# Two inner norms applied behind the products, in a transformer step on one core

## Chip, core and metric

The kernel runs on one core of a Trainium2 chip. TensorE multiplies into PSUM, VectorE (DVE) and ScalarE (ACT) do the elementwise work, GpSimd (POOL) a few selects, and SyncE (SP) issues nearly all loads. Each engine works through its own queue of instructions in order; they meet through semaphores. The metric is the device time of one execution in microseconds.

## What is computed

One inference step of a two-layer decoder on 288 tokens (256 of a prompt, 8 x 4 of running sequences), width 1024, fp32. Layer 0 is sparse attention and a dense SwiGLU, layer 1 a gated gMLP and a top-2-of-8 expert SwiGLU. Cut to what matters here:

```python
def rms_norm(x, g):
    y = xf * lax.rsqrt(jnp.mean(xf * xf, axis=-1, keepdims=True) + EPS)
    return (y * g.astype(jnp.float32)).astype(x.dtype)
def swiglu(h, w_gate, w_up, w_down):
    return (jax.nn.silu(h @ w_gate) * (h @ w_up)) @ w_down
def gmlp_mixer(h, w_in, ln_g, ln_b, w_s, b_s, w_out):
    u, v = jnp.split(jax.nn.gelu(h @ w_in, approximate=False), 2, axis=-1)
    v = layer_norm(v, ln_g, ln_b)
    ...
    return (u * mixed.reshape(B, T, GM_WIDTH)) @ w_out, v
xp = xp + op.reshape(B, S, -1) @ attn_w_out[j]
xp = xp + swiglu(rms_norm(xp, norm_ffn[i]), ffn_w_gate[j], ffn_w_up[j], ffn_w_down[j])
op, _ = gmlp_mixer(rms_norm(xp, norm_mix[i]), ...)
```

The two inner norms are the one ahead of the dense SwiGLU (n = 1) and the one ahead of the gMLP (n = 2).

## The kernel before

The residual stream `xT` lies transposed, 8 chunks of 128 features by 288 tokens. A dense product is made in three: each operand is split into a high part (rounded to `fp32r`) and a low part (the rest), and `three()` (L1660) adds high x high, high x low and low x high. `project_split` makes a block of 128 output columns from 8 chunks, 24 products. `project_tokens_split` has the tokens as the stationary side, and works through a quarter of the weights (2 chunks) at a time for three tiles of tokens, 18 products.

Weights come in tiles of 2 MB through a ring of 7 slots. A tile has four quarters. ScalarE copies the head of a quarter into one of `WD` = 3 buffers `wd` (`heads_before`, L754), as soon as TensorE has read the quarter three before it (`d_used`); VectorE subtracts it in place to get the tail (`tails_before`, L1150). Where the calls `heads_before(n)` and `tails_before(n)` stand in each engine's program sets the order of this work against the rest. `F0`, `FD0`, `GV0`, `GU0`, `GO0` number the first quarters of gate and up, down, the gMLP's v and u halves and its output.

Results land in six PSUM banks in turn (`A`), named ("wo", m) for the attention output, ("fg", f) and ("fu", f) for gate and up, ("fd", m) for down, ("gv", m, half), ("gu", c), ("mix", g); `room` makes TensorE wait until the bank six names earlier is freed. The sums of squares use two more banks (`B`).

An inner norm, before: VectorE adds each block to `xT` (`residual`, L1390). After the last, ScalarE and VectorE square half of the stream each (L791, L1164), `ssq` (L1643) sums over features with eight fp32 products with `ones`, ScalarE takes the root into `rt` (L793), VectorE the reciprocal (L1166) and then, chunk by chunk, weight times norm (L1168, into `hL`), ScalarE the high part `hT_r` (`h_heads`), VectorE the low part `hL_r` (`h_tail_of`, L1158). Only then has TensorE its operand. In the FFN loop ScalarE makes Silu of the gate block from PSUM (L969) and VectorE the product with the up block (L1407), whose high and low parts are `hh` and `hhl_r` (L1400). Ahead of the second norm ScalarE issues five loads of parameters (L979 to L983). In the gMLP the v half goes through Gelu (L992), statistics (L1429), roots (L1003) and a layer norm on VectorE (L1448 to L1451) while TensorE makes the u half, whose Gelu is at L1000. The mix adds its bias at L1458.

## Time and profile before

| | us |
|---|---|
| median of 3 runs (lowest, highest) | 1683.6 (1681.77, 1691.64) |
| the profiled execution | 1692.52 |
| its span, first to last instruction | 1690.8 |
| busy: TensorE, its weight loads | 1618.4 (96%), 1377.8 (81%) |
| busy: VectorE, ScalarE, GpSimd | 1237.8 (73%), 986.6 (58%), 54.5 (3%) |
| mean granted TensorE clock | 0.971 |

The attention stages fill the first 303 us, the FFN runs to 530, the gMLP to 646, and the eight experts take the rest. A timeline row is start, length, engine, line, operation, output and inputs; the bracket at its end says how long the engine had idled before it, and what released it. L1660 is the line of all split products, L754 of all copies on ScalarE, whose output tells them apart.

### The profile page before, as it was taken

The page shows a single profiled execution, that of the slowest core. Times are in us where ns is not written, and L with a number is a line of the kernel's source. Part 1 is how long each engine was busy: PE and PEld are TensorE (multiplying, and loading weights), DVE is VectorE, ACT ScalarE, POOL GpSimd, SP SyncE. Part 2 cuts the span into 40 slices and gives each one's busy share as a digit, 9 for nine tenths or more (in the row PEclk, how much of TensorE's full clock was granted, in tenths as well). Part 3 has the DMA queues.
Part 4 walks back from the last instruction along what each step waited for, and adds up shares of the span by engine and source line. Part 5 has one row for each costly group of instructions (what it writes and reads, how often), then busy time and mean ns, then how long its engine had stood idle before and what let it go on. Part 6 is the DMA issues. An engine that isn't in the chain of part 4 may idle for free.

```text
span 1690.8 us, 22113 instructions
## 1 busy us (share of the span) xinstructions
PE 1618.4 (96%) x8441; PEld 1377.8 (81%) x8441; DVE 1237.8 (73%) x1168; ACT 986.6 (58%) x933; POOL 54.5 (3%) x62
## 2 busy tenths in 40 slices
PE   7998989899996998899999999999999999999998
PEld 6886978799996787788888888888888888888886
DVE  4586353455533484888998988998998988988986
ACT  2443342344432445677777767767767777777774
POOL 3520000000000000000000000000000000000000
PEclk9999689999998999999999999999999999999999
DMA  7194236153645232699999999999999999999980
GB/s 235 69 349 157 100 123 227 50 175 126 223 150 200 84 119 100 250 350 346 361 356 345 373 349 345 371 346 343 380 344 343 367 356 342 362 356 350 365 292 29
DMA packets 194264, 444.17 MB, mean 263 GB/s; under 512 B 10841, under 2 KB 13947, under 8 KB 194203
## 3 DMA queue, kind: packets, MB, share of 16 engines
q1 hardware_dynamic: 190082, 436.91, 71.5%
q10 hardware_dynamic: 4120, 6.42, 1.1%
q8 instruction: 41, 0.67, 0.2%
q14 instruction: 21, 0.16, 0.0%
HBM read 439.57 MB, written 3.74 MB: 262 GB/s over the span
## 4 chain that ended last, share of the span: by engine, by line
PE 90%; DVE 6%; ACT 1%; issue 1%; ACTq 1%; DMA 0%; DVEq 0%
PE bank L1660 20%; PE bank L2065 12%; PE bank L2067 12%; PE bank L2066 12%; PE bank L2075 6%; PE bank L2077 6%; PE bank L2076 6%; PE bank L1652 3%; PE bank L1831 2%; PE bank L2083 1%; PE bank L2038 1%; DVE rt L1292 1%; PE bank L1821 1%; PE bank L2053 1%; PE bank L2054 1%
## 5 line engine op out<-in xcount | busy, mean ns | idle before, releaser
L1499 DVE TENSOR_TENSOR wql<-ring,wqh 128x2048 fp32r<-128x2048 f32 x336 | 767.6, 2288 | 112.4 <-ACT wqh L754 109.3
L754 ACT ACTIVATE wqh<-ring 128x2048 fp32r<-128x2048 f32 x336 | 646.2, 1924 | 261.0 <-PE bank L2067 172.2
L2065 PE MATMUL bank<-wqh,xgh 128*128 128x512 f32 x896 | 357.5, 399 | 4.2 <-DVE wql L1499 2.5
L2067 PE MATMUL bank<-wqh,xgl 128*128 128x512 f32 x896 | 350.8, 392 | 0.0
L2066 PE MATMUL bank<-wql,xgh 128*128 128x512 f32 x896 | 350.2, 391 | 0.0
L1150 DVE TENSOR_TENSOR ring_r<-ring,wd 128x1024 fp32r<-128x1024 f32 x90 | 109.9, 1224 | 140.5 <-ACT wd L754 140.5
L2065 PEld LDWEIGHTS bank<-wqh,xgh 128*128 128x128 f32 x896 | 169.1, 189 | 38.6 <-DVE wql L1499 3.4
L2067 PEld LDWEIGHTS bank<-wqh,xgl 128*128 128x128 f32 x896 | 169.0, 189 | 36.5
L2066 PEld LDWEIGHTS bank<-wql,xgh 128*128 128x128 f32 x896 | 169.3, 189 | 33.1
L1660 PE MATMUL bank<-hT_r,ring_r 128*128 128x288 f32 x608 | 180.8, 297 | 0.0
L2075 PE MATMUL bank<-wqh,heTh 128*128 128x512 f32 x448 | 175.1, 391 | 1.9 <-DVE heTl L1499 1.9
L2077 PE MATMUL bank<-wqh,heTl 128*128 128x512 f32 x448 | 175.0, 391 | 0.0
L2076 PE MATMUL bank<-wql,heTh 128*128 128x512 f32 x448 | 174.8, 390 | 0.0
L754 ACT ACTIVATE wd<-ring 128x1024 fp32r<-128x1024 f32 x90 | 94.9, 1057 | 117.2 <-PE bank L1660 117.1
L1660 PE MATMUL bank<-hT_r,wd 128*128 128x288 f32 x480 | 143.9, 300 | 8.5 <-DVE hL_r L1158 5.8
L1660 PE MATMUL bank<-hL_r,wd 128*128 128x288 f32 x480 | 143.4, 299 | 0.0
L1660 PEld LDWEIGHTS bank<-hT_r,ring_r 128*128 128x128 f32 x608 | 116.0, 191 | 0.0
L1660 PEld LDWEIGHTS bank<-hT_r,wd 128*128 128x128 f32 x480 | 92.5, 193 | 11.9 <-issue 6.4
L2075 PEld LDWEIGHTS bank<-wqh,heTh 128*128 128x128 f32 x448 | 84.5, 189 | 19.7 <-DVE wql L1499 2.2
L2076 PEld LDWEIGHTS bank<-wql,heTh 128*128 128x128 f32 x448 | 84.5, 189 | 17.6
L2077 PEld LDWEIGHTS bank<-wqh,heTl 128*128 128x128 f32 x448 | 84.4, 188 | 17.6
L1660 PEld LDWEIGHTS bank<-hL_r,wd 128*128 128x128 f32 x480 | 92.0, 192 | 0.0
(331 smaller groups left out, 1906.2 us busy)
## 6 DMA issues: line engine op xcount, KB each, us to landing
ring<-in_moe_w_gate SPq DMA_DIRECT2D x56, 2048.0 KB, 8.2
ring<-in_moe_w_up SPq DMA_DIRECT2D x56, 2048.0 KB, 8.1
ring<-in_moe_w_down SPq DMA_DIRECT2D x56, 2048.0 KB, 8.3
ring<-in_attn_w_in SPq DMA_DIRECT2D x7, 2048.0 KB, 10.2
ring<-in_ffn_w_gate SPq DMA_DIRECT2D x5, 2048.0 KB, 8.6
ring<-in_ffn_w_up SPq DMA_DIRECT2D x5, 2048.0 KB, 7.8
ring<-in_cache_k SPq DMA_DIRECT2D x16, 512.0 KB, 13.0
ring<-in_cache_v SPq DMA_DIRECT2D x16, 512.0 KB, 5.6
```

Of the source, the lines that this page charges most:

```text
L754: return nc.scalar.activation(dst, src, ACT.Copy)
L1150: v.tensor_tensor(in_tile(n, ring_r), in_tile(n), its_heads(n).bitcast(F32), ALU.subtract)\
L1499: return v.tensor_tensor(dst, src, head.bitcast(F32), ALU.subtract)
L1652: last = mm(A.ap(group)[0:width, 0:ncols], tile[:, c, col:col + width], rhs[:, c, 0:ncols], start=(c == 0), stop=(c == k - 1))
L1660: return mm(out, w, x, **flags) if weights_stay else mm(out, x, w, **flags)
L1831: last = mm(B.ap("st")[:, c0:c0 + TS], KT[:, n % 2, h, :], qT[:, h, NP + TS * b:NP + TS * b + TS], start=True, stop=True)
L2065: mm(bank, xgh[:, k, :], w_h[:, part], start=(k == 0), stop=False)
L2066: mm(bank, xgh[:, k, :], w_l[:, part], start=False, stop=False)
L2067: last = mm(bank, xgl[:, k, :], w_h[:, part], start=False, stop=(k == KD - 1))
L2075: mm(bank, heTh[:, left], w_h[:, part], start=first, stop=False)
L2076: mm(bank, heTh[:, left], w_l[:, part], start=False, stop=False)
L2077: last = mm(bank, heTl[:, left], w_h[:, part], start=False, stop=final)
```

## The change

A row's norm is a factor per token, and a product is linear in it. So the change feeds the products with the stream times weight only, not divided, and multiplies the results. For the SwiGLU both results are multiplied by `rt` on VectorE, the gate ahead of Silu. For the v half the factor lies along partitions, so it is the `scale` of the Gelu on ScalarE (`rk`); for the u half VectorE multiplies by `rt` ahead of Gelu. High and low parts of the weighted stream are made behind each residual add: the high part on ScalarE straight from `xT`, the low part on VectorE in one instruction. ScalarE squares each chunk, VectorE keeps a running sum in `rt`, and TensorE sums over features with one product with `ones`, put after the first block of the stage (for n = 2 with three small ones that give the factor per token row). Line numbers below are not those of before.

```diff
-        def squares_and_root(n, xt_ready):
...
+        def raw_heads(n, name, chunks, dst):
+            for m in chunks:
+                act.wait_ge(*A.freed((name, m)))
+                nc.scalar.activation(dst[:, m, :], xT[:, m, :], ACT.Copy, scale=gT[:, 8 * n + m:8 * n + m + 1])\
+                  .then_inc(h_head, 1)
+                k = KD * (n - 1) + m
+                if k >= 2:
+                    act.wait_ge(usum_ok, k - 1)
+                nc.scalar.activation(usq[:, m % 2, :], xT[:, m, :], ACT.Square).then_inc(usq_ok, 1)
...
-        squares_and_root(1, A.freed(("wo", KD - 1)))
-        h_heads(h_ready, KD)
+        raw_heads(1, "wo", range(KD), hU)
+        nc.scalar.activation(rk[0:1, 3:4], epst[0:1, 0:1], ACT.Sqrt)
         for f in range(NFB):
...
             heads_before(F0 + 2 * f + 1 + WD)
+            if f == 0:
+                act.wait_ge(*B.full(("ssq", 1)))
+                nc.scalar.activation(rt[:], B.ap(("ssq", 1))[:, 0:T], ACT.Sqrt, bias=epst[:, 0:1], scale=1.0 / D)\
+                  .then_inc(b_act, 1)
+            act.wait_ge(*A.freed(("fg", f)))
+            nc.scalar.activation(sg[:, f % 2, :], sg[:, f % 2, :], ACT.Silu).then_inc(silu_ok, 1)
...
         hidden_head(NFB - 1)
+        heads_before(first_of["fd", 1, 0] + WD - 1)
+        raw_heads(2, "fd", range(4), hT_r)
+        heads_before(GV0 + WD - 1)
+        raw_heads(2, "fd", range(4, KD), hT_r)
         heads_before(GV0 + WD)
+        nc.scalar.activation(rk[0:1, 3:4], epst[0:1, 0:1], ACT.Sqrt)
...
-        squares_and_root(2, A.freed(("fd", KD - 1)))
-        h_heads(h_ready, 2 * KD)
+        heads_before(GV0 + QU + WD - 1)
+        act.wait_ge(*B.full(("ssq", 2)))
...
+        act.wait_ge(ln_ok, 1)
+        nc.scalar.activation(mv[:, 0:2, 2:3], mv[:, 0:2, 1:2], ACT.Sqrt, bias=epst[:, 0:1])
...
         for c in range(KD):
             heads_before(GU0 + c + 1 + WD)
-            act.wait_ge(*A.full(("gu", c)))
...
+            act.wait_ge(*A.freed(("gu", c)))
+            nc.scalar.activation(gu[:, c, :], gu[:, c, :], ACT.Gelu).then_inc(gelu_ok, 1)
...
+        def raw_tail(n, m, heads):
+            turned[0] += 1
+            dve.wait_ge(h_head, turned[0])
+            v.scalar_tensor_tensor(out=hL_r[:, m, :], in0=xT[:, m, :], scalar=gT[:, 8 * n + m:8 * n + m + 1],
+                                   in1=heads[:, m, :].bitcast(F32), op0=ALU.mult, op1=ALU.subtract).then_inc(h_tail, 1)
...
+                v.tensor_tensor(rt[:], rt[:], usq[:, m % 2, :], ALU.add).then_inc(usum_ok, 1)
...
         for f in range(NFB):
+            dve.wait_ge(*A.full(("fg", f)))
...
+            v.tensor_tensor(sg[:, f % 2, :], A.ap(("fg", f))[:, 0:T], rt[:], ALU.mult).then_inc(a_dve, 1)
             tails_before(F0 + 2 * f + 1 + WD)
-            dve.wait_ge(*A.full(("fu", f)))
-            dve.wait_ge(*A.freed(("fg", f)))
-            v.tensor_tensor(hhl[:, f, :], sg[:, f % 2, :], A.ap(("fu", f))[:, 0:T], ALU.mult).then_inc(a_dve, 1)
             if f >= 1:
                 hidden_tail(f - 1)
+            dve.wait_ge(*A.full(("fu", f)))
+            v.tensor_tensor(hhl[:, f, :], A.ap(("fu", f))[:, 0:T], rt[:], ALU.mult).then_inc(a_dve, 1)
+            dve.wait_ge(*A.freed(("fu", f)))
+            dve.wait_ge(silu_ok, f + 1)
+            v.tensor_tensor(hhl[:, f, :], hhl[:, f, :], sg[:, f % 2, :], ALU.mult).then_inc(prod_ok, 1)
             tails_before(F0 + 2 * f + 2 + WD)
         hidden_tail(NFB - 1)
-        tails_before(first_of["fd", 1, 0] + WD)
...
+        tails_before(first_of["fd", 1, 0] + WD - 1)
+        for half in range(2):
+            for m in range(4 * half, 4 * half + 4):
+                residual("fd", m)
+                if m > 4 * half:
+                    raw_tail(2, m - 1, hT_r)
+            raw_tail(2, 4 * half + 3, hT_r)
+            if half == 0:
+                tails_before(GV0 + WD - 1)
...
-        def ssq(n):
+        def sum_of_squares(n):
+            bank = B.ap(("ssq", n))
             B.room(pe, ("ssq", n))
...
+            pe.wait_ge(usum_ok, KD * n)
+            last = mm(bank[:, 0:T], ones[:], rt[:], start=True, stop=True)
...
-            for m in range(4):
-                A.room(pe, ("fd", 4 * half + m))
...
                         for m in range(4):
+                            if f == 0:
+                                A.room(pe, ("fd", 4 * half + m))
```

Where the instructions stand, at three places. First VectorE from the end of the attention output on, before (L1390 residual, L1164 squares, L1168 and L1158 the normed chunk and its low part):

```order
L1150 TENSOR_TENSOR ring_r<-ring,wd 128x8x128 x3
L1390 TENSOR_TENSOR xT<-xT,bank 128x288 x8
L1164 TENSOR_TENSOR hT<-xT 128x1152
L1166 RECIPROCAL rt<-rt 128x288
L1168 SCALAR_TENSOR_TENSOR hL<-xT,gT,rt 128x288 x2
L1158 TENSOR_TENSOR hL_r<-hL,hT_r 128x288
```

and now, from the last residual add (L1410) to the second pair of the FFN loop (L1186 low part, L1194 running sum, L1172 tail of a quarter, L1433 gate times norm, L1438 up times norm, L1441 product with Silu):

```order
L1410 TENSOR_TENSOR xT<-xT,bank 128x288
L1186 SCALAR_TENSOR_TENSOR hL_r<-xT,gT,hU 128x288
L1194 TENSOR_TENSOR rt<-rt,sg 128x288
L1186 SCALAR_TENSOR_TENSOR hL_r<-xT,gT,hU 128x288
L1194 TENSOR_TENSOR rt<-rt,sg 128x288
L1172 TENSOR_TENSOR ring_r<-ring,wd 128x8x128
L1421 RECIPROCAL rt<-rt 128x288
L1433 TENSOR_TENSOR sg<-bank,rt 128x288
L1438 TENSOR_TENSOR hhl<-bank,rt 128x288
L1441 TENSOR_TENSOR hhl<-hhl,sg 128x288
L1172 TENSOR_TENSOR ring_r<-ring,wd 128x8x128
```

The low part of chunk 6 stands behind the last residual add, and the reciprocal behind one more tail.

Second, ScalarE from the end of the down projection on, before:

```order
L754 ACTIVATE wd<-ring 128x1024 x22
L979 DMA wr<-in_moe_w_router 128x8x8
L980 DMA wsr<-in_gm_w_s 128x8x128
L981 DMA lng<-in_gm_ln_g 128x1024
L982 DMA lnb<-in_gm_ln_b 128x1024
L983 DMA bsb<-in_gm_b_s 128x1024
L791 ACTIVATE hT<-xT 128x1152
L793 ACT_TABLE_LOAD
L793 ACTIVATE rt<-bank,epst 128x288
L754 ACTIVATE hT_r<-hL 128x288 x8
L754 ACTIVATE wd<-ring 128x1024 x4
L992 ACT_TABLE_LOAD
```

and now, from the last weighted copy (L798) and square (L803):

```order
L798 ACTIVATE hT_r<-xT,gT 128x288
L803 ACTIVATE sg<-xT 128x288
L760 ACTIVATE wd<-ring 128x1024
L992 ACT_TABLE_LOAD
L992 ACTIVATE rk<-epst 1x1
L996 DMA wr<-in_moe_w_router 128x8x8
L997 DMA wsr<-in_gm_w_s 128x8x128
L998 DMA lng<-in_gm_ln_g 128x1024
L999 DMA lnb<-in_gm_ln_b 128x1024
L1000 DMA bsb<-in_gm_b_s 128x1024
L760 ACTIVATE wd<-ring 128x1024 x3
L1005 ACTIVATE rk<-bank,epst 128x2
```

The five DMAs stand behind the weighted copies, between the head of quarter 2 of the v half and those of quarters 3, 4 and 5.

Third, VectorE in the gMLP after the statistics, now (L1492 u block times norm, L1481, L1484, L1486 the layer norm's three steps; before, the nine of them and three tails came in a row, with no L1492):

```order
L1492 TENSOR_TENSOR gu<-bank,rt 128x288
L1172 TENSOR_TENSOR ring_r<-ring,wd 128x8x128
L1484 TENSOR_TENSOR gv<-gv,lng 128x1024
L1486 TENSOR_TENSOR gv<-gv,lnb 128x1024
L1492 TENSOR_TENSOR gu<-bank,rt 128x288
L1172 TENSOR_TENSOR ring_r<-ring,wd 128x8x128
L1481 TENSOR_SCALAR gv<-gv,mv 128x1024
L1484 TENSOR_TENSOR gv<-gv,lng 128x1024
```

Each tail now stands behind two steps of the norm at most, and the roots on ScalarE stand ahead of its first head of this stage.

## Rows read from the trace of the kernel before

**Rows 1.** The page's second part, granted clock in 40 slices
```profile
PEclk9999689999998999999999999999999999999999
```
**Rows 2.** The timeline around the first inner norm
```profile
303.36 0.45 DVE L1390 TENSOR_TENSOR xT<-xT,bank 128x288 f32<-128x288 f32 x1 [3.43 <-PE bank L1652]
...
305.35 5.81 PE L1643 MATMUL bank<-hT,ones 128*128 128x288 f32 x16 [2.03 <-DVE hT L1164]
...
311.73 1.95 DVE L1166 RECIPROCAL rt<-rt 128x288 f32<-128x288 f32 x1 [6.53 <-ACT rt L793]
...
315.12 0.51 DVE L1168 SCALAR_TENSOR_TENSOR hL<-xT,gT,rt 128x288 f32<-128x288 f32 x1
...
315.35 0.38 PE L1660 MATMUL bank<-hT_r,wd 128*128 128x288 f32 x1 [4.19 <-DVE hL_r L1158]
...
324.42 1.06 ACT L754 ACTIVATE wd<-ring 128x1024 fp32r<-128x1024 f32 x1 [1.65 <-PE bank L1660]
...
324.49 0.45 DVE L1407 TENSOR_TENSOR hhl<-sg,bank 128x288 f32<-128x288 f32 x1 [0.46 <-PE bank L1660]
```
**Rows 3.** The chain of waits in order of time: start, length, what, instructions
```profile
37.35 3.47 PE bank L1732 x32
...
270.35 32.98 PE bank L1652 x128
...
320.05 171.43 PE bank L1660 x1301
...
586.47 0.87 PE bank L1975 x8
```
**Rows 4.** The timeline between the halves of the down projection
```profile
491.56 1.06 ACT L754 ACTIVATE wd<-ring 128x1024 fp32r<-128x1024 f32 x1 [2.12 <-PE bank L1660]
...
494.86 0.37 PE L1660 MATMUL bank<-hh,wd 128*128 128x288 f32 x1 [3.26 <-DVE xT L1390]
```
**Rows 5.** The timeline around the second inner norm
```profile
534.91 2.80 ACTq L981 DMA_DIRECT2D lng<-in_gm_ln_g  x1
...
538.73 1.16 ACT L791 ACTIVATE hT<-xT 128x1152 f32<-128x1152 f32 x1 [7.63 <-issue]
...
539.99 6.36 PE L1643 MATMUL bank<-hT,ones 128*128 128x288 f32 x16 [9.91 <-ACT hT L791]
...
551.33 0.76 PE L1660 MATMUL bank<-wd,hT_r 128*128 128x512 f32 x1 [4.99 <-DVE hL_r L1158]
...
557.17 1.06 ACT L754 ACTIVATE wd<-ring 128x1024 fp32r<-128x1024 f32 x1 [1.89 <-PE bank L1660]
...
561.33 1.06 ACT L754 ACTIVATE wd<-ring 128x1024 fp32r<-128x1024 f32 x1 [3.11 <-PE bank L1660]
```
**Rows 6.** The timeline of the gMLP's u half
```profile
588.57 1.28 DVE L1429 BATCH_NORM_STATS2 bn<-gv 128x6 f32<-128x512 f32 x2
...
600.73 0.81 DVE L1448 TENSOR_SCALAR gv<-gv,mv 128x1024 f32<-128x1024 f32 x1
...
601.38 1.28 ACT L1000 ACT_TABLE_LOAD   x1
...
601.57 1.23 DVE L1450 TENSOR_TENSOR gv<-gv,lng 128x1024 f32<-128x1024 f32 x1
...
602.67 0.41 ACT L1000 ACTIVATE gu<-bank 128x288 f32<-128x288 f32 x1
...
605.34 0.37 PE L1660 MATMUL bank<-hT_r,wd 128*128 128x288 f32 x1 [1.86 <-DVE ring_r L1150]
...
619.65 0.41 DVE L1458 TENSOR_TENSOR hL<-bank,bsb 128x256 f32<-128x256 f32 x1
```
**Rows 7.** Busy time by stretch: length, PE, PEld, DVE, ACT, POOL, clock, DMA share
```profile
606.00:609.50 3.50, 3.50 (x17) 3.50 (x16) 3.47 (x4) 0.00 (x0) 0.00 (x0) 0.52 0.41 150
690.00:1000.00 310.00, 310.00 (x1407) 255.84 (x1405) 274.72 (x173) 224.40 (x154) 0.00 (x0) 1.00 0.98 355
```
**Rows 8.** The timeline, a later weighted copy of one chunk
```profile
634.11 0.54 ACT L1025 ACTIVATE uT<-xT,gT 128x288 f32<-128x288 f32 x1 [1.66 <-DVE xT L1390]
```

More of the change, by code:

```diff
@@ L1395, in _ @@
             residual("wo", m)
-        norm(1, A.freed(("wo", KD - 1)), hL)
+            if m:
+                raw_tail(1, m - 1, hU)
+        raw_tail(1, KD - 1, hU)
+        tails_before(F0 + 1 + WD)
+        dve.wait_ge(*B.freed(("ssq", 1)))
+        v.reciprocal(rt[:], rt[:]).then_inc(r_ok, 1)
+        dve.wait_ge(r_ok, 1)
         def hidden_tail(f):
@@ L1455, in _ @@
+        for _ in norming:
+            pass
         for g in range(8):
```

147 lines of the change are left out of this document (76 added, 71 removed).

## Prediction

> **What bounds the kernel now.** I read the page first. The line of the granted clock is near full speed but for the fifth and sixth slice, ahead of the change [rows 1], so the body runs on a busy TensorE and only stretches where it stops can be won. Next the chain of waits in order of time: between 270 and 645 us it is nearly all TensorE. The stretches of it give prices per product: 64 fp32 products (two instructions each) of the attention output take 32.98 us, 0.52 each; 1301 split products take 171.43 us, 0.132 each, so a block of 24 is 3.16 us; 16 fp32 products of 8 columns take 3.47 us, 0.22 each [rows 3]. Then the timeline for the places where TensorE idles. There are five in reach of the change.
>
> A: the first inner norm. The last residual add starts at 303.36, TensorE does eight fp32 products with `ones` for 5.81 us, ScalarE takes the root, VectorE a reciprocal of 1.95 us, and TensorE stands still for 4.19 us ahead of its first split product. The first product of gate and up comes on VectorE at 324.49 [rows 2]. So 21.1 us pass from the end of the attention output (303.33) to the end of the second FFN block (324.42), which itself holds two blocks, 6.3 us.
>
> B: between the halves of the down projection, 3.26 us idle. The fifth block of 128 columns waits until VectorE has made one more low part and then all four residual adds [rows 4].
>
> C: the second inner norm. TensorE stops at 530.08 (539.99 less 9.91), because ScalarE issues five DMAs (one of them for 2.80 us) before it squares, at 538.73. Then come 6.36 us of sums and 4.99 us idle until 551.33 [rows 5]. The next stage, eight quarters of 18 products, ends at 586.47 [rows 3]; undisturbed a quarter takes 4.17 us, as the head copies of 557.17 and 561.33 stand apart [rows 5].
>
> D: the u half of the gMLP, where VectorE normalises v between its low parts: 1.86 us idle at 605.34, then the clock at 0.52 for 3.5 us [rows 6, 7].
>
> After that comes the expert stage, with TensorE busy 310 of 310 us at full clock while the DMA engines are busy 98% [rows 7]. Each transfer there waits for a ring slot that the products free, so the stage should shift as a whole.
>
> **The change, part by part.** Times below count from the end of the TensorE work ahead of a place. A semaphore takes about 0.05 us (324.42 to 324.49 has one). A VectorE row that waits for nothing starts some 0.08 us before its predecessor ends. The weighted copy on ScalarE is 0.54 us [rows 8]. The square of a chunk I take as 0.44 us, as a copy less its scale operand; the bounds are 0.41 and 0.54. A product and subtraction in one VectorE instruction is 0.51, an add 0.45, the residual's [rows 2].
>
> *A.* Per chunk VectorE has residual add, low part and running sum, 0.45 + 0.51 + 0.45 = 1.4 us; ScalarE has 0.54 + 0.44. An attention output block takes 8 x 0.52 = 4.1 us, so chunks 0 to 6 hide, except that the tail of chunk 6 stands behind residual 7 in VectorE's queue (order rows above). That tail ends at 0.9, chunk 7's at 1.8. TensorE asks for chunk 6 at 18 x 0.132 = 2.4 and for chunk 7 at 2.8: no wait. Block 1 ends at 3.16, one fp32 product with `ones` replaces eight, 0.52, the second block ends at 6.84. Behind it: head of quarter 3 3.15 to 4.2, root to 4.7, tail to 5.45, reciprocal to 7.4, three products with the norm and the gate until 8.9, head and tail of quarter 4 until 10.7, wanted at 13.2. So A goes from 21.1 to 6.8: **14.3 us**.
>
> *FFN loop.* Two more VectorE products per block pair, 22 x 2 x 0.45 = 20 us of work, are costed at nothing: they lie beside 6.32 us of TensorE per pair, in which VectorE then has two low parts of 1.23 and four products and differences of 0.45, 4.3 us. The latest item is the tail of the quarter behind the Silu product. After the up block is full (3.16): scaled up 3.65, product with Silu 4.1, and the tail (its head done at 4.2) 5.4, wanted at 6.32: slack 0.9 us. Silu itself is done at 1.5 and not waited for. Without this cover each us of lateness would cost 22 us.
>
> *B.* The tail that stood ahead of the adds is now behind them, and the room is asked for by block. Residuals 0 and 1 end at 0.5 and 0.9; TensorE comes to blocks 6 and 7 at 0.8 and 1.2. Late next is the low part of the third quarter: ScalarE's four weighted copies and squares follow VectorE's 1.3 us per chunk and end at 4.55, head to 5.6, tail to 6.85; wanted at 6.32. So 3.26 becomes 0.55: **2.7 us**.
>
> *C.* The bank of the third token tile waits for residual 4: start at 0.5. Quarters 0 and 1 need chunks 0 to 3, made at B; chunks 4 to 7 are done at 5.2, wanted from 8.9. ScalarE then has the head of quarter 2 (to 5.6), the table and the dummy root (to 7.1), the DMAs (4.9, to 12.0) and only then the head of quarter 3, 13.05, tail 14.3. TensorE wants it at 0.5 + 3 x 4.17 = 13.0: a new wait of 1.3. Sums: 0.52 + 3 x 0.22 = 1.2. Root, reciprocals (1.95 + 0.3) and `rk` are ready for Gelu by 23 and hidden by the second half; the first bank that Gelu frees is wanted at 36. So C takes 0.5 + 33.4 + 1.3 + 1.2 = 36.4 instead of 586.47 - 530.08 = 56.4: **20.0 us**.
>
> The DMA issue is the term with far bounds. It is at least 2.5 us (2.80 less any waiting, the four short ones stay) and at most 4.9 plus the 8 us that the ring tile issued at the same moment could hold the queue; I take 4.9 as measured, with the same traffic around it. The low bound removes the wait (gain 1.3 more), the high one makes it some 8.
>
> *Table load.* The dummy root costs 1.28 + 0.2 us here. In the rows the table load of 1.28 us at 601.38 was followed by its activation at 602.67 at once [rows 6]. The Trainium skill, "ScalarE: Activation LUTs", section "What ACT_TABLE_LOAD costs", adds a drain of about 1.38 us to every switch; by that rule the head of quarter 3 would be 1.4 us later still and C 18.6. This case's trace doesn't show the drain, so the sum goes by the trace.
>
> *D.* VectorE is the bound between the end of the v stage (0) and the first mix add: 33.2 us in before (619.65 - 586.47). Now: statistics from 2.1 to 6.4 (1.28 a pair, plus 0.16 as I take it for each aggregate), one product, then a wait for the two roots and the next head (8.1), tail and reciprocals to 9.65, and nine norm rows (0.81 and twice 1.23 three times over, 9.8) [rows 6], seven products (2.7), seven tails (8.1) and the sample weights (nine tiny instructions, 1.0 as I take it): 31.1, overlaps of 0.08 taken off. All eight products of TensorE find their low part ready; it waits at the mix instead. Gain **2.0 us**, bounds 0 and 3.5 (1.86 and the slow clock).
>
> Sum 14.3 + 2.7 + 20.0 + 2.0 = 39.0 us. The profiled execution took 1692.5 us (span 1690.8), so 1653.5; it is 8.9 above the median of the runs, which gives 1683.6 - 39.0 = **1644.6 us**.
>
> **The rivals.**
> 1. *A wait takes the place of the sums (gain 27 to 35 us, about 1653).* Place: quarter 3 of C, behind ScalarE's DMAs, and the clock behind each short stop. For it: a stop of 1.86 us was followed by 3.5 us at 0.52, which cost 1.7 us [rows 6, 7]; three new short stops (B, C, mix) at that price cost 5, and a queue held 3 us longer costs 3. Against it: the stop of 3.26 us at B has no slow rows behind it. By the Trainium skill, "TensorE: Matmul & The Clock Gate", section "A second HAM failure mode: psum-queue depth-cycling", frequent micro-idling makes the clock swing between its levels; the wait rows here bear that out once in two.
> 2. *The expert stage gives it back (within 1%).* For it: DMA at 98% from 690 to 1000 us. If the weights were the bound, the earlier start would win nothing beyond the tiles already in the ring. Against it: TensorE idles 0 us there; transfers are paced by slots it frees. Time then between 1668 and 1683.
> 3. *Slower: the FFN's VectorE queue.* The tail stands behind a wait for ScalarE's Silu. If round trip and queue end more than 0.9 us later than worked out, each pair loses the rest; at 0.9 + 39.0 / 22 = 2.7 us late the gain is gone, at 3.7 the time is 1683.6 + 22 = 1706. For it: VectorE's share rises from half of the stage to two thirds. Against it: its rows are 0.45 us and Silu is done 2 us before.
>
> **How the numbers follow.** Forecast (gain 35 to 42) 0.72, rival 1 0.20, rival 2 0.05, rival 3 beyond no gain 0.02, a smaller loss there 0.01. The range reaches from the low bound of the DMAs and of D (-1.3, -1.5, and 4 for the state of the chip, since three runs lie 10 us apart) to rival 1: 1637 to 1657. About 1% is what a measurement of this kernel can tell from no change: faster 0.93 (gain above 17), same 0.05, slower 0.02.
>
> **What would show it.** TensorE should pass from the attention output to the FFN without a stop, with one `ones` product between its first two blocks; the gMLP's v stage should start within 1 us of the down projection and pause once, before its fourth quarter, ahead of which ScalarE's queue shows the DMAs; the FFN loop should keep 0.132 us a product (if not: rival 3); the expert stage should keep TensorE busy throughout (if not: rival 2). The prediction is wrong if the low clock follows the new stops for more than 3.5 us each.

## The result, and the profile after

| | before | after |
|---|---|---|
| median us (runs) | 1687.62 (1681.77, 1683.6, 1691.64, 1692.54) | 1642.54 (1641.32, 1642.12, 1642.96, 1643.46) |
| ratio | | 0.9734, 95% interval 0.9708 to 0.976 |
| profiled execution, its span | 1692.52, 1690.8 | 1642.12, 1640.4 |
| mean granted clock | 0.971 | 0.984 |

The kernel is faster; the forecast was 1644.6 us, with a range of 1637 to 1657. The kernel before was run 25 more times beside the experiments (medians 1683.47, 1684.47 and 1684.84), so its median in the table is some 4 us high; against 1684 the change is worth 42 us, a ratio of 0.975. One thing has to be taken out of the difference of the two spans, 50.4 us, before it is read. The attention output starts at 260.50 us in the profile of after and at 270.35 in that of before, in code that the change does not touch (`rk` moves its tiles by 32 bytes, too). That is 9.85 us, and the clock accounts for it: the fifth and sixth slice of the page (169 to 254 us in before, 164 to 246 in after) stand at 6 and 8 in before [rows 1] and at 9 and 8 in after. Up to that start the mean granted clock is 0.91 in before and 0.95 in after, and 270.35 x 0.91 and 260.50 x 0.95 are 246 and 247 us of full clock. The other 40.5 us lie behind that point, where the change is. From here on, "behind attention" is the span less the start of the attention output: 1420.45 us in before, 1379.9 in after.

The page of after, its busy times and its granted clock:

```profile
PE 1594.5 (97%) x8419; PEld 1359.7 (83%) x8419; DVE 1257.1 (77%) x1220; ACT 993.0 (61%) x951; POOL 54.6 (3%) x62
...
PEclk9999989999999998999999999999999999999999
```

The chain of waits of after in order of time (start, length, what, instructions), around the first inner norm and then around the second:

```profile
294.09 3.18 PE bank L1718 x24
297.27 0.49 PE bank L1696 x2
297.76 14.25 PE bank L1718 x107
```

```profile
500.00 21.95 PE bank L1718 x112
521.95 0.48 PE bank L1696 x2
522.44 0.50 PE bank L1700 x6
522.94 16.57 PE bank L1718 x71
```

Where [rows 2] has eight products with `ones`, a stop of 4.19 us and the first split product at 315.35, there is now one product (two instructions, L1696) between the first two blocks, and no stop. Where [rows 5] has stops of 9.91 and 4.99 us around 6.36 us of sums, the second chain runs through: one product of 288 columns and three of 8 (L1700). From 294 to 566.57 us TensorE never stands still for more than 0.04 us, and its granted clock is 1.00; in before it is 0.96 from 303.3 to 586.3 us and 0.88 in C alone, so a part of the gains at A and C is clock that the stops no longer cost. The one new stop is at the mix, where the forecast had it. In the timeline of after:

```profile
567.48 0.38 PE L2050 MATMUL bank<-wsT,gv 128*128 128x128 f32 x1 [0.90 <-DVE gv L1486]
```

The clock stays at 1.00 behind it, up to 600 us.

Stage by stage, from the timelines of both (us):

| stretch | before | after | gain | forecast |
|---|---|---|---|---|
| A: end of the attention output to end of the second FFN block | 21.1 | 6.8 | 14.3 | 14.3 |
| rest of the FFN loop, and down | | | 1.3 | 2.7 (B), loop 0 |
| of it B, the stop between the halves | 3.26 | 0 | 3.3 | 2.7 |
| C: end of down to the transposes | 56.2 | 34.3 | 22.0 | 20.0 |
| D: transposes to the first mix addition | 33.3 | 30.8 | 2.5 | 2.0 |

C and D are taken here from the first transpose of the timeline, 586.30 in before and 539.57 in after, 0.17 us ahead of where the chain [rows 3] has it. The table leaves one loss: B alone gave 3.3, the whole stretch 1.3, so the loop took 2 us more. It shows in VectorE's scaling of each gate block, here two pairs in a row of after's timeline:

```profile
348.98 0.46 DVE L1433 TENSOR_TENSOR sg<-bank,rt 128x288 f32<-128x288 f32 x1 [0.95 <-PE bank L1718]
...
355.38 0.46 DVE L1433 TENSOR_TENSOR sg<-bank,rt 128x288 f32<-128x288 f32 x1 [0.95 <-PE bank L1718]
```

A pair takes 6.40 us; in before, 6.29 on average over 17 pairs. TensorE stops in neither, so each product has become slower, 0.1333 us instead of 0.1311.

The timeline of after around the second norm, ScalarE and the DMA issues (ACTq and SPq are the queues of ScalarE and SP that issue them):

```profile
505.33 0.37 SPq L641 DMA_DIRECT2D ring<-in_moe_w_gate  x1
...
507.83 0.54 ACT L798 ACTIVATE hT_r<-xT,gT 128x288 fp32r<-128x288 f32 x1 [0.29 <-DVE xT L1410]
507.98 0.41 ACTq L996 DMA_DIRECT2D wr<-in_moe_w_router  x1
508.27 0.43 ACT L803 ACTIVATE sg<-xT 128x288 f32<-128x288 f32 x1
508.42 0.60 ACTq L997 DMA_DIRECT2D wsr<-in_gm_w_s  x1
508.61 1.05 ACT L760 ACTIVATE wd<-ring 128x1024 fp32r<-128x1024 f32 x1
509.05 3.93 ACTq L998 DMA_DIRECT2D lng<-in_gm_ln_g  x1
509.67 1.28 ACT L992 ACT_TABLE_LOAD   x1
510.96 0.20 ACT L992 ACTIVATE rk<-epst 1x1 f32<-1x1 f32 x1
513.00 0.46 ACTq L999 DMA_DIRECT2D lnb<-in_gm_ln_b  x1
513.49 0.45 ACTq L1000 DMA_DIRECT2D bsb<-in_gm_b_s  x1
514.04 2.01 ACT L760 ACTIVATE wd<-ring 128x1024 fp32r<-128x1024 f32 x2 [2.88 <-PE bank L1718]
```

Down ended at 505.30. The forecast had these in a row: square, head, table and dummy root until 7.1 us behind that, then 4.9 us of issues, then the head of quarter 3 at 12.0. The rows show the issues beside the engine's work, and that head at 8.74.

### The profile page after: what moved, and what is told of

Read it like the earlier page. It is cut to its first block, busy times and chain, and to the rows that moved or that the text cites. A ratio compares the mean times of both kernels' runs of the same rounds, so it can differ in the third digit from the quotient of the medians.

```text
span 1640.4 us, 22161 instructions
## 1 busy us (share of the span) xinstructions
PE 1594.5 (97%) x8419; PEld 1359.7 (83%) x8419; DVE 1257.1 (77%) x1220; ACT 993.0 (61%) x951; POOL 54.6 (3%) x62
## 4 chain that ended last, share of the span: by engine, by line
PE 91%; DVE 6%; issue 1%; ACT 1%; ACTq 0%; DMA 0%; DVEq 0%
PE bank L1718 20%; PE bank L2125 13%; PE bank L2127 12%; PE bank L2126 12%; PE bank L2135 6%; PE bank L2137 6%; PE bank L2136 6%; PE bank L1710 3%; PE bank L1889 2%; PE bank L2143 1%; PE bank L2098 1%; DVE rt L1312 1%; DVE ring_r L1172 1%; PE bank L2113 1%; PE bank L2114 1%
## 5 line engine op out<-in xcount | busy, mean ns | idle before, releaser
L760 ACT ACTIVATE wqh<-ring 128x2048 fp32r<-128x2048 f32 x336 | 646.4, 1925 | 260.5 <-PE bank L2127 171.9
L1172 DVE TENSOR_TENSOR ring_r<-ring,wd 128x1024 fp32r<-128x1024 f32 x90 | 109.9, 1224 | 81.3 <-ACT wd L760 79.8
L1718 PE MATMUL bank<-hU,wd 128*128 128x288 f32 x352 | 104.6, 297 | 0.0
L1718 PE MATMUL bank<-hU,ring_r 128*128 128x288 f32 x352 | 103.5, 294 | 0.0
L1718 PE MATMUL bank<-hT_r,ring_r 128*128 128x288 f32 x256 | 75.9, 296 | 0.0
L1718 PEld LDWEIGHTS bank<-hU,ring_r 128*128 128x128 f32 x352 | 66.3, 188 | 0.0
```

What stands on the lines that cost most here:

```text
L760: return nc.scalar.activation(dst, src, ACT.Copy)
L1172: v.tensor_tensor(in_tile(n, ring_r), in_tile(n), its_heads(n).bitcast(F32), ALU.subtract)\
L1718: return mm(out, w, x, **flags) if weights_stay else mm(out, x, w, **flags)
```

## The experiments

Four questions were open: whether the gains belong to the two norms separately, what made the loop's products slower, which steps spared the waits that the forecast expected, and how much room the FFN's VectorE queue has. "Pair" is the mean distance of 17 pairs of the loop by VectorE's low parts of the hidden blocks.

| kernel | us | attention output starts | behind attention | to the first down product | pair | down | C | D |
|---|---|---|---|---|---|---|---|---|
| before | 1692.5 | 270.35 | 1420.45 | 186.10 | 6.294 | 73.62 | 56.23 | 33.35 |
| after | 1642.1 | 260.50 | 1379.90 | 174.68 | 6.400 | 70.12 | 34.27 | 30.83 |
| n1_only | 1674.2 | 261.69 | 1410.51 | 174.67 | 6.400 | 75.07 | 56.05 | 33.49 |
| n2_only | 1659.9 | 264.13 | 1394.07 | 187.54 | 6.400 | 70.13 | 34.22 | 30.83 |
| rk_pad | 1648.1 | 265.96 | 1380.34 | 173.90 | 6.346 | 70.27 | 34.38 | 30.85 |
| pad_head | 1653.6 | 273.02 | 1378.88 | 172.92 | 6.346 | 70.26 | 34.39 | 29.88 |
| dma_late | 1643.1 | 261.40 | 1380.00 | 174.78 | 6.400 | 70.12 | 34.27 | 30.84 |
| banks_together | 1652.1 | 267.42 | 1382.98 | 174.70 | 6.400 | 70.57 | 35.16 | 30.84 |
| sum_first | 1653.4 | 266.23 | 1385.47 | 177.22 | 6.400 | 70.11 | 34.27 | 30.83 |
| extra4 | 1641.9 | 260.34 | 1379.86 | 174.07 | 6.400 | 70.12 | 34.27 | 30.83 |
| extra8 | 1644.5 | 263.23 | 1379.57 | 174.07 | 6.358 | 70.12 | 34.27 | 30.83 |
| ring_later | 1641.5 | 259.83 | 1379.87 | 174.77 | 6.400 | 70.12 | 34.27 | 30.83 |
| hl_moved | 1651.3 | 267.76 | 1381.84 | 173.54 | 6.346 | 70.25 | 34.25 | 30.83 |
| best | 1639.2 | 260.94 | 1376.56 | 173.58 | 6.347 | 69.85 | 34.37 | 29.86 |

The time is that of the profiled execution; dma_late, banks_together, sum_first, extra8, ring_later and hl_moved were run only once. The start of the attention output wanders between 259.8 and 273.0 with the clock in the stages ahead of it, so totals of single executions differ by up to 13 us for nothing that the kernels do differently. The columns from "to the first down product" on repeat to some tenths of a us, but for one or two us where a phase of low clock falls into them. "Behind attention" does not: it holds the stages behind the first mix addition too, in whose instructions the kernels here do not differ, and they took between 1068.9 us (best) and 1073.0 (sum_first; hl_moved 1072.9), 1070.0 in after. So up to 4 us in that column are no work of an edit.

### One norm at a time

n1_only takes the first norm and the FFN loop of the changed kernel and leaves norm 2, mid-down and the gMLP as before; n2_only is the reverse:

```diff
 n1_only
-        raw_heads(2, "fd", range(4), hT_r)            # ACT, and its counterparts on DVE and PE
+        squares_and_root(2, A.freed(("fd", KD - 1)))
+        h_heads(h_ready, KD)
 n2_only
-        raw_heads(1, "wo", range(KD), hU)
+        squares_and_root(1, A.freed(("wo", KD - 1)))
+        h_heads(h_ready, KD)
```

> Only the first norm and the FFN loop are the changed kernel's; the second norm, the mid-down place and the gMLP are those of the kernel before. Theory (the gains are separate and add): the hand-over into the FFN stays at 6.8 us (21.1 before), the mid-down wait is back at 3.26 us, the second norm takes 56.4 us again. Against the kernel before that is 14.3 us less, and 2.2 us more if a gate and up pair takes 6.40 us as in the changed kernel, not 6.29: about 12 us of 1,687 us, ratio 0.993, on top of what the unchanged attention stages vary by (10 us between two profiled runs). Rival (the first norm's gain was really the attention stages' 9.9 us): the place still shows near 21 us. On the pair: both the new FFN queue and the 32-byte tile rk are in this kernel, so 6.40 us is expected by either cause.

> Only the second norm (with mid-down and the gMLP) is the changed kernel's; the first norm and the FFN loop are those of before. The tile rk of 32 bytes a partition is in it, so all tiles allocated behind it stand 32 bytes further on, as in the changed kernel. Theory (gains add): the first norm takes 21.1 us again, mid-down near 0 (3.26 before), the second norm 34.3 us (56.4 before), the u half 30.8 us (33.2 before): 27.7 us less than before. On the gate and up pair: if the 6.40 us (6.29 before) come from the place of the tiles in memory, this old loop shows 6.40 and 2.2 us of the gain are lost; if they come from the new loop's VectorE and ScalarE work, it shows 6.29. Ratio to before 0.984 to 0.985, without what the attention stages vary by.

n1_only: 1675.19 us median of 6, ratio 0.9953 (0.9932 to 0.9974); n2_only: 1659.87 of 4, ratio 0.987 (0.9848 to 0.9893). Each alone is within 2% of before, and both totals gained less than expected (0.993, and 0.984 to 0.985). The stretches come out as expected, but for the old first norm in n2_only and the second half of down in n1_only. n1_only has the chain of after at its first norm (295.26 3.19, 298.46 0.48, 298.94 on) and the old second norm; its place to the first down product is after's to 0.01 us, 11.4 us less than before. n2_only has C and D of after. The old first norm takes 19.6 us in it, not 21.1, as two phases of low clock fall otherwise, so 1.5 of A's 14.3 us hang on where the clock falls in the profile of before.

Behind attention the gains are 9.9 and 26.4 us, 36.3 together, against 40.5 for both. The missing 4.2 has two large parts. The slow pair is in both kernels and is counted twice; it is worth 22 x 0.106 = 2.3 us. And n1_only has a phase of low clock in the second half of down, which costs it 1.45 us (75.07 less 73.62 for down). With both the sum is 40.0. The rest is wander that nearly cancels: the attention output takes 0.8 us longer in n2_only than in before, the gap behind it, ahead of the first split product, is 1.7 us shorter, and the stages behind the first mix addition gave 1.1 us in after and took 0.3 in these two together. So the gains add up, as far as this wander of 1 to 2 us lets one see. The windows of n1_only, then of before, over the two halves (length, PE, PEld, DVE, ACT, POOL, clock, DMA share, GB/s):

```profile
436.40:471.40 35.00, 35.00 (x265) 34.87 (x264) 14.77 (x14) 12.11 (x12) 0.00 (x0) 1.00 0.59 215
474.80:511.40 36.60, 36.60 (x264) 36.40 (x264) 12.70 (x12) 10.60 (x10) 0.00 (x0) 0.96 0.44 159
```

```profile
494.90:530.00 35.10, 35.10 (x264) 34.94 (x264) 12.68 (x12) 10.61 (x10) 0.00 (x0) 1.00 0.46 164
```

The same stop of 3.27 us stands ahead of the second half in both. It was followed by a slow phase in one execution and not in the other, so the stops also cost something that differs from run to run. The changed kernel has no such stop.

### Why the products of the FFN loop slowed down

n2_only decides the first half of this: its loop is the old one, word for word, and its pair takes 6.400 us, not 6.294. So the new loop's work on VectorE and ScalarE isn't needed for 6.400. What n2_only shares with the changed kernel is the tile `rk` of 32 bytes a partition, behind which all later tiles move up. Three kernels move them otherwise:

```diff
 rk_pad
-    rk = sb("rk", [P, 4], stack=trunk)
+    rk = sb("rk", [P, 16], stack=trunk)
 best (and the head moved, below)
+    rk = sb("rk", [P, 32], stack=trunk)
 hl_moved
     wd = sb("wd", [P, WD, 1024], F32R, stack=dense)
+    sb("hl_pad", [P, 24], stack=dense)
     hL, hL_r = both("hL", [P, KD, T], dense)
```

> The changed kernel with rk 64 bytes a partition instead of 32, so that the tiles behind it stand 64 bytes further on than before, not 32. If the place of the tiles (32 bytes off a multiple of 64, before; on one, in the changed kernel) sets the time of a product, a gate and up pair takes 6.29 us as before, and the kernel is about 2.2 us faster than the changed one. If the new loop's extra work on VectorE and ScalarE, or reading its streams from another tile (hU), does it, the pair stays at 6.40 us. Norm places as in the changed kernel: 6.8, 0, 34.3, 30.8 us.

> The changed kernel with 96 unused bytes a partition between the tile of the weights' heads (wd) and that of the stream's low parts (hL): wd stays where it is in the changed kernel (on a multiple of 128 bytes), hL and the tiles behind it stand 96 bytes further, as they stood to 128 in the kernel before. Gate and up pairs so far: wd and hL 96 bytes over a multiple of 128 in the kernel before 6.294 us; 32 bytes over 6.346; on it 6.400. If the place of the weights' tile decides: 6.40 us. If that of the stream's low parts decides: 6.29 us. If both count: between.

| kernel | loop | byte of `wd`, modulo 128 | of `hL` | of the tile with the stream's heads | pair |
|---|---|---|---|---|---|
| before | old | 96 | 96 | 32 | 6.294 |
| n2_only | old | 0 | 0 | 32 | 6.400 |
| after | new | 0 | 0 | 0 | 6.400 |
| rk_pad | new | 32 | 32 | 32 | 6.346 |
| hl_moved | new | 0 | 96 | 96 | 6.346 |
| best | new | 96 | 96 | 96 | 6.347 |

hl_moved leaves `wd` where the changed kernel has it and still gets what rk_pad gets, and best, which moves `wd` too, gets no more, so the place of the weights' heads doesn't count. What the faster kernels share is that `hL`, and what lies behind it (`hh`, `hhl`, `sg` and, in the new loop, `hU`), stands 32 bytes off a multiple of 64. All of these on a multiple of 64 cost 0.05 us a pair in the new loop and 0.11 in the old; in all 22 pairs 1.2 and 2.3 us. Restoring the place wins back only half.

Which of these tiles it is, isn't shown, since no kernel moves one alone. `hL` is the only one besides `wd` that TensorE reads in the old loop, but the trace doesn't point at the products that read it: over 104 us of the loop, from before to n2_only, the mean distance from the start of a product to the start of the next grows by 0.9 ns (131.7 to 132.6) behind those that read `hL`, by 4.1 ns (129.1 to 133.2) behind those that read `hT_r` with `wd`, and by 1.5 ns (132.6 to 134.1) behind those with `ring_r`. The rule doesn't carry over to down either, whose products read `hh` and `hhl_r`: without its stop down takes 70.4 us in before and 69.9 in best, both with these tiles at 96, and 70.1 in after with them at 0. What makes the other 0.053 us of the new loop (the tile `hU` instead of `hT`, its place, or VectorE's traffic) was not tried, and the theory of rk_pad, 6.29, fell, as did that of best. Why a place in memory matters to a product at all, no row shows.

By totals none of this can be told: rk_pad took 1647.47 us, median of 4, ratio 0.979 (0.9766 to 0.9814), more than the changed kernel, with its attention output 5.5 us later.

### What spared the expected waits

The forecast had three waits that after doesn't show: 0.55 us at B, 0.5 at the start of C, 1.3 ahead of its quarter 3. One kernel tests the step that was left out, the early start of the residual additions, and one the place of the sum:

```diff
 banks_together
-                            if f == NFB - 1:
-                                last.then_inc(a_full, 1)
+                        if f == NFB - 1:
+                            last.then_inc(a_full, 4)
 sum_first
+            if f == 0:
+                sum_of_squares(1)
             project_split(("fg", f), F0 + 2 * f, hL_r, KD + 1 if f == 0 else None, hU)
-            if f == 0:
-                sum_of_squares(1)
```

> The four down blocks of a half signal only when the last product of all four has been issued; in the changed kernel each signals at its own last product, three, six and nine products (0.4, 0.8, 1.2 us) sooner. Theory (the residual additions begin before TensorE is done with the half, which the forecast had left out): mid-down gets a wait of TensorE of up to 0.5 us back, as forecast, and the second norm one of 0.3 to 0.9 us at its start, 0.3 to 1.4 us in all. Rival (the additions' early start is not what saved the forecast waits): no stop appears at either place.

> The product with ones that sums the first norm's squares stands ahead of the first gate block, not behind it. Theory (its place behind the block hides the chunk sums of VectorE): TensorE waits at the head of the FFN for the last square and sum, 1.5 to 2.5 us, and the place takes 8.3 to 9.3 us instead of 6.8 from its end of the attention output to the end of the first up block's products' due time; pairs stay at 6.40 us. Rival (the sum would have been ready, its place is of no matter): no stop over 0.3 us.

The timeline of after, then of banks_together, at mid-down:

```profile
469.34 0.81 DVE L1410 TENSOR_TENSOR xT<-xT,bank 128x288 f32<-128x288 f32 x2
...
474.55 2.36 DVE L1172 TENSOR_TENSOR ring_r<-ring,wd 128x1024 fp32r<-128x1024 f32 x2 [0.30 <-ACT wd L760]
```

```profile
477.30 0.82 DVE L1410 TENSOR_TENSOR xT<-xT,bank 128x288 f32<-128x288 f32 x2 [0.94 <-PE bank L1718]
...
482.51 3.50 DVE L1172 TENSOR_TENSOR ring_r<-ring,wd 128x1024 fp32r<-128x1024 f32 x3 [0.29 <-ACT wd L760]
483.36 0.29 PE L1718 MATMUL bank<-hh,ring_r 128*128 128x288 f32 x1
483.79 0.41 PE L1718 MATMUL bank<-hh,wd 128*128 128x288 f32 x1
```

In after the additions start 1.0 us before TensorE ends the half (470.32). With one common signal VectorE stands 0.94 us for it, the low part of the third quarter comes at 483.7, and TensorE loses 0.3 us there (0.43 from one product to the next, not 0.13; the whole of down 0.45). The start of C gets a stop of 0.71 us, and C takes 35.16, 0.9 more. The theory holds at both places, and the wait ahead of quarter 3 doesn't come back.

sum_first stands 2.23 us, as expected, and needs 2.54 us more to the first down product. Its timeline, the head of the FFN:

```profile
302.09 0.72 PE L1696 MATMUL bank<-rt,ones 128*128 128x288 f32 x2 [2.23 <-DVE rt L1194]
```

Behind the first block the same product waits for nothing.

### The DMAs in ScalarE's queue

```diff
 dma_late
-        nc.scalar.activation(rk[0:1, 3:4], epst[0:1, 0:1], ACT.Sqrt)
+        nc.scalar.activation(rk[0:1, 3:4], epst[0:1, 0:1], ACT.Sqrt).then_inc(root2, 1)
+        act.wait_ge(root2, 1)
 ring_later
-            over = (...) if part < 2 else A.full(("fd", 4 * half + 3))
+            over = (...) if part < 2 else A.full(("fd", 3) if half == 0 else ("gv", 2, 0))
```

> In the changed kernel the five DMAs that ScalarE starts behind the second norm's squares were issued from 507.98 us on, while its engine still ran copies and squares until 509.7 and the table load until 510.96. Here ScalarE waits for its dummy root before it issues them. Theory (in the changed kernel they were issued ahead of the work that stands before them in the queue, and so cost the path less than forecast): the issues start only behind the table load, near 511, take 5 to 6 us, the head of the third weight quarter begins 2.5 to 3 us later than 514.0, and TensorE stands 1.4 to 2 us ahead of the third quarter, so that the stretch from the end of the down projection to the transposes becomes 35.6 to 36.3 us (34.3 in the changed kernel). Rival (issues take their place in the queue either way): nothing moves, 34.3 us.

The rival, that nothing moves, has the time right and the reason wrong. The issues did start late, but the long one shrank:

```profile
511.96 0.20 ACT L993 ACTIVATE rk<-epst 1x1 f32<-1x1 f32 x1
512.19 0.40 ACTq L998 DMA_DIRECT2D wr<-in_moe_w_router  x1
512.63 0.60 ACTq L999 DMA_DIRECT2D wsr<-in_gm_w_s  x1
513.26 0.79 ACTq L1000 DMA_DIRECT2D lng<-in_gm_ln_g  x1
514.08 0.45 ACTq L1001 DMA_DIRECT2D lnb<-in_gm_ln_b  x1
514.56 0.45 ACTq L1002 DMA_DIRECT2D bsb<-in_gm_b_s  x1
515.11 2.01 ACT L761 ACTIVATE wd<-ring 128x1024 fp32r<-128x1024 f32 x2 [2.95 <-PE bank L1720]
```

Down ended at 506.30, so `lng` was through 7.75 us behind it; in after 7.68 (3.93 us long), in banks_together 7.61 (2.85), in before 7.64 (2.80 [rows 5]). The end is fixed, and the start is not. At the end of down SP issues a ring tile of 2048 KB, and the page gives 8.3 us from issue to landing. ring_later takes that tile away from there:

> The 2 MB ring tile that SP loads at the end of the down projection (505.33 in the changed kernel, landed 8.3 us later) waits for the first half of the v stage, some 17 us more. In ten kernels the issue of the layer norm's first row (lng) ended 7.6 to 7.8 us behind the end of the down projection, whether it had begun 3.0, 3.7, 4.8 or 7.0 us behind it, and took 0.79 us where it began latest. Theory (the issue is held until that ring tile is through): here it takes about 0.8 us, all five issues 2.8 us, and ScalarE makes the head of the third quarter right behind its dummy root, 5.9 to 6.3 us behind the end of the down projection, not 8.74. TensorE's times don't move (34.3 us from the down projection to the transposes). Rival (the issue waits for something of ScalarE's own, its table load or the two transfers started ahead of it): it takes 3 to 4 us as in the changed kernel.

```profile
507.39 0.41 ACTq L996 DMA_DIRECT2D wr<-in_moe_w_router  x1
507.69 0.43 ACT L803 ACTIVATE sg<-xT 128x288 f32<-128x288 f32 x1
507.83 0.60 ACTq L997 DMA_DIRECT2D wsr<-in_gm_w_s  x1
508.02 1.05 ACT L760 ACTIVATE wd<-ring 128x1024 fp32r<-128x1024 f32 x1
508.46 0.60 ACTq L998 DMA_DIRECT2D lng<-in_gm_ln_g  x1
...
510.49 1.04 ACT L760 ACTIVATE wd<-ring 128x1024 fp32r<-128x1024 f32 x1
```

`lng` takes 0.60 us, and the head of quarter 3 comes 5.8 us behind down, not 8.7. So the issue was held until the ring tile was nearly through. At that moment the timeline of ring_later has no issue on SP's queue.

The chain of the forecast, table and dummy root ahead of the issues, is what dma_late has, and it has no wait either. Its root ends 5.86 us behind down, not at 7.1, since the additions begin early; and its five issues take 2.8 us, not 4.9, since the end of the long one is fixed. With 4.9 us the low part would have ended at 5.86 + 4.9 + 1.06 + 1.23 = 13.05, against the 12.4 at which TensorE wants it: an estimate from these rows, which leaves 0.6 us of the forecast 1.3 to the length of the issues and 0.7 to the early start. In ring_later TensorE's times don't move, since in after too the low part is in time: the head ends at 515.1, the low part at 516.4, and quarter 3 is wanted at 505.3 + 3 x 4.15 = 517.7. The rows of after and ring_later also show that a DMA issue doesn't wait for the ACTIVATEs ahead of it: `wr` is issued while the last copy runs and the last square has not begun. That an engine works through its queue in order thus holds for its own work, and not for the DMA issues between.

### The room in the FFN's VectorE queue

```diff
 extra4 (extra8: 0:8)
+            v.tensor_tensor(hT[:, 0:4, :], xT[:, 0:4, :], xT[:, 0:4, :], ALU.mult)
             v.tensor_tensor(hhl[:, f, :], A.ap(("fu", f))[:, 0:T], rt[:], ALU.mult).then_inc(a_dve, 1)
```

> VectorE gets one further product of 128x1152 (1.36 us in the kernel before) in every pair of the FFN loop, ahead of the scaling of the up block; it writes a tile that nobody reads before it is written anew. Theory (the weight quarter's low part behind the product with the Silu is what is late next, with 0.95 us of slack: it ends at 348.0 and TensorE comes to it at 348.98): the low part is 0.4 us late in each of 22 pairs, a pair takes 6.8 us in place of 6.40, and the kernel 9 us more than the changed kernel. Rival A (the slack is larger, since the queue catches up elsewhere): pair 6.40 us, time unchanged. Rival B (the delay goes round through the freed buffers and adds up): a pair takes more than 7.2 us, 18 us or more in all.

> As extra4, with a further product of 128x2304 (about 2.7 us) in every pair of the FFN loop. Extra4 cost nothing, since the low part made behind the Silu product is wanted one block later than the forecast had it (352.18, ended 348.03: 4.15 us of slack). Theory (what is left as a bound is VectorE's load of a pair: two low parts of 1.23 and four operations of 0.45 are 4.3 us, with overlaps 4.2): 4.2 + 2.7 = 6.9 us is over the 6.40 us of TensorE, a pair takes 6.8 to 7.2 us, 9 to 17 us more in the loop than in the changed kernel. Rival (a lateness of more than 0.9 us counts at once, extra4 just escaped): each pair loses 1.8 us or more, 8.2 us a pair.

extra4: 1643.07 us median of 4, ratio 0.978 (0.972 to 0.984), and behind attention 1379.86, against 1379.90 of the changed kernel. It costs nothing, where 9 us were expected; rival A had the time right. By the forecast, the low part behind the product with Silu is wanted when the next gate block is done, 3.2 us behind the up block. In the timeline of extra4 the up block is full at 345.0, so that is 348.2, and the low part ends at 347.14 + 1.22 = 348.36; TensorE's products go on at 348.14, 348.28 and 348.41 without a stop. With three tiles of heads (`WD`) the quarter made there is that of the gate block after the next one, wanted 3.2 us later still, at 351.4, and in after at 352.1 for an end at 348.0. VectorE's timeline of extra8, one whole pair:

```profile
348.28 2.55 DVE L1438 TENSOR_TENSOR hT<-xT 128x2304 f32<-128x2304 f32 x1
350.75 0.45 DVE L1439 TENSOR_TENSOR hhl<-bank,rt 128x288 f32<-128x288 f32 x1
351.23 0.46 DVE L1442 TENSOR_TENSOR hhl<-hhl,sg 128x288 f32<-128x288 f32 x1
351.61 1.22 DVE L1172 TENSOR_TENSOR ring_r<-ring,wd 128x1024 fp32r<-128x1024 f32 x1
352.74 0.45 DVE L1433 TENSOR_TENSOR sg<-bank,rt 128x288 f32<-128x288 f32 x1
353.11 1.22 DVE L1172 TENSOR_TENSOR ring_r<-ring,wd 128x1024 fp32r<-128x1024 f32 x1
354.24 0.45 DVE L1426 TENSOR_TENSOR hhl_r<-hhl,hh 128x288 fp32r<-128x288 f32 x1
354.61 2.55 DVE L1438 TENSOR_TENSOR hT<-xT 128x2304 f32<-128x2304 f32 x1
```

VectorE is busy without a break, and a pair of it takes 354.61 - 348.28 = 6.33 us, just under TensorE's 6.40; behind attention stands 1379.57. So the time expected of extra8 was too high, and its rival's too: the added product takes 2.55 us, not 2.7, and the seven rows of a pair, 6.80 us by their durations, overlap by 0.07 us each. So VectorE has about 2.5 us of room in each pair, and the queue could not have lost time.

### A version that is a little shorter

```diff
 pad_head, best
+        heads_before(GU0 + 1 + WD)
         act.wait_ge(ln_ok, 1)
         nc.scalar.activation(mv[:, 0:2, 2:3], mv[:, 0:2, 1:2], ACT.Sqrt, bias=epst[:, 0:1])
```

> As rk_pad, and in the gMLP ScalarE makes the head of the next weight quarter ahead of its wait for the row statistics and the two roots, not behind them. In the changed kernel that head ran at 546.54 us, behind the wait that ended at 546.15, and VectorE stood 1.18 us for it (to 547.61). Theory (VectorE's queue sets the end of the u half): the 1.18 us go, the roots' table load ends 1.3 us behind the statistics as before, so the u half takes 0.8 to 1.2 us less, 29.6 to 30.0 us from the transposes to the first mix addition (30.8 in the changed kernel). Rival (the roots are what the queue waits for next): VectorE then stands as long for the roots and 30.5 us or more stay.

> The changed kernel with rk 128 bytes a partition, so that wd and hL stand 96 bytes over a multiple of 128 as in the kernel before, and with the head of the gMLP's fourth weight quarter ahead of the wait for the row statistics. Theory (a product's time goes by the place within 128 bytes): a pair takes 6.29 us, 2.3 us less in the loop; the u half takes 29.9 us as measured with the head moved (30.8 in the changed kernel); 3.2 us less than the changed kernel in the stages, median near 1640 apart from what the attention stages vary by. Rival (the place within 256 bytes or another measure decides): pair 6.35 or 6.40 us.

The timeline of after, then of pad_head, on VectorE around the statistics:

```profile
546.04 0.39 DVE L1492 TENSOR_TENSOR gu<-bank,rt 128x288 f32<-128x288 f32 x1
547.61 1.22 DVE L1172 TENSOR_TENSOR ring_r<-ring,wd 128x1024 fp32r<-128x1024 f32 x1 [1.18 <-ACT wd L760]
```

```profile
557.07 0.39 DVE L1493 TENSOR_TENSOR gu<-bank,rt 128x288 f32<-128x288 f32 x1
557.39 1.20 DVE L1173 TENSOR_TENSOR ring_r<-ring,wd 128x1024 fp32r<-128x1024 f32 x1
```

VectorE's 1.18 us go and D is 0.95 us shorter, as expected (pad_head: 1648.88 us, median of 4, ratio 0.9786, 0.9764 to 0.9808). Best is 3.3 us shorter behind attention than the changed kernel (1376.56 to 1379.90), but 1.1 of that lies behind the first mix addition, where its instructions do not differ. The stages give 2.2 us, not the 3.2 expected: 1.1 up to the first down product, since a pair takes 6.347 us and not 6.29, 0.3 in down and 1.0 in D, less 0.1 in C. The total can't tell that: best took 1639.2, 1642.2, 1650.85, 1651.14 and 1651.52 us, median 1650.85, ratio 0.9785 (0.9758 to 0.9811), with the attention stages in it. Its fastest run is the fastest of all here. That it is shorter than the changed kernel is shown by the stages of one execution of each alone.

## Why the prediction was right, point by point

- **What bounds.** That only stops of TensorE can be won held: stops and sums are gone, and all stretches of products kept their length to some tenths of a us but for the loop.
- **A.** 14.3 us forecast and measured, the chain as described. 1.5 of it depends on where phases of low clock fall (n2_only).
- **B.** 2.7 forecast, 3.3 measured. The step that failed is "residuals 0 and 1 end at 0.5 and 0.9", counted from TensorE's end: each bank is full at its own last product, and the additions begin 1.0 us ahead (banks_together). The third quarter's low part, "6.85; wanted at 6.32", comes in time for the same reason.
- **C.** 20.0 forecast, 22.0 measured. Of the 2.0 us, 0.5 is the wait at the start, which fell for the same reason, 1.3 the wait ahead of quarter 3, and 0.1 the sums (1.08 us for 1.2). The step that failed is "the DMAs (4.9, to 12.0)": the issues don't queue behind the engine's work, and the long one ends with the ring tile (dma_late, ring_later). The root is early too, so of the 1.3 some 0.7 go back to the residuals. The pause "once, before its fourth quarter", a sign that the forecast named, did not show. The forecast had named a hold by that tile as its high bound and put it behind the other work, worth some 8 us; it was there and cost nothing, since it ran beside that work.
- **Table load.** Also here an activation follows its table load at once: 295.51 and 1.28, then 296.81; 524.73 and 1.28, then 526.02. The rule that the prediction quoted from the Trainium skill, "ScalarE: Activation LUTs", section "What ACT_TABLE_LOAD costs", with a drain of 1.38 us, is not borne out by this kernel.
- **D.** 2.0 forecast, 2.5 measured (31.1 and 30.8 for the new length); VectorE is the chain as described, and TensorE waits at the mix, for 0.90 us.
- **FFN loop.** "Costed at nothing" was right for the work and wrong in its reason. The slack of 0.9 us was mis-sized: the low part is wanted one block later (slack 4.1 us), and the load of the queue, 2.5 us under the limit, bounds it (extra4, extra8). What the forecast left out is that a new tile moves others, worth 2.3 us in the old loop (n2_only). The sign "the FFN loop should keep 0.132 us a product (if not: rival 3)" failed, at 0.1333, and not by rival 3: VectorE's queue was not late.
- **Sum.** 39.0 forecast; 40.5 behind attention. 14.3 + 3.3 + 22.0 + 2.5 less 2.0 for the loop is 40.1; the attention output took 0.6 us longer in after (33.6 to 33.0), and the stages behind the first mix addition 1.1 less, which no term had. From the median 1683.6 that is 1643, and 1642.54 was measured. That the forecast lies within 2.1 us of it is luck in part: 3.1 us too little at B, C and D stand against the 2.0 that the loop lost, and in kernels with the same code up to there the attention output starts between 259.8 and 267.8 us, by the clock; after's 260.5 is near the low end.
- **Rivals.** 1: no wait took the place of the sums, and the one new stop, at the mix, has no slow phase behind it. 2: the expert stage gave nothing back: from the first mix addition to the end 1070.0 us in after, 1071.15 in before, with kernels of the same code there between 1068.9 and 1073.0. 3: excluded by extra8.

## What to carry over

A sum over all chunks can be taken off the path by linearity: scale behind the product, and let one product make the sum between two blocks that don't need it; its place counts beside its length (2.5 us here, sum_first). Count the start of the next engine's work from the signal of each bank, not from the end of the stage. And when a change adds a tile, compare a product's rate in stages that it doesn't touch: a few bytes of padding may be part of the result. Where an untouched stage wanders by microseconds from one execution to the next, compare stages and not totals.

## What the runs showed of the hardware

- A DMA issue of ScalarE's queue goes out while earlier ACTIVATEs still run or wait to run (507.98 beside 507.83 and 508.27), unless a semaphore orders them.
- The issue of `lng`, a row broadcast to 128 partitions, 512 KB, takes 0.60 us with no ring tile under way (ring_later), and 2.80 to 3.98 us when it begins within 5 us of the issue of one of 2048 KB on SP's queue; it then ends 7.4 to 7.7 us behind that issue, whenever it began (0.79 us where it began 6.9 us behind, in dma_late).
- A split product of 288 columns takes 0.1333 us or 0.1311 in the old loop (n2_only, before), and 0.1333 or 0.1322 in the new one (after, hl_moved), at the same full clock and without a stop, by where in memory `hL` and the tiles behind it stand (a multiple of 64 bytes, or 32 off it). Which of them counts, and why, is open.
- The same stop of 3.27 us was followed by a granted clock of 0.96 over the next 36.6 us in one execution (n1_only), and of 1.00 over the next 35.1 us in another (before).
